# Dilated attention in a two-layer decoder trunk: near products wait for near values only, value loads and bias tables handled anew, products five steps behind their scores

## The chip, the cores and the metric

The kernel runs on the 8 NeuronCores of one Trainium2 chip. Each core computes one of the 8 batch elements alone; the cores share nothing but the memory's bandwidth. The metric is the device time in microseconds of the slowest core.

## The reference

```python
for layer in range(2):
    mod = silu(c) @ w_mod[layer] + b_mod[layer]            # shift, scale, gate for both sub-layers
    h = rms_norm(x) * (1 + scale_m) + shift_m              # (2048, 1024) per batch element
    q, k, v, rq, rk, rv, rg = split(h @ w_in[layer])       # 3 x 512, 2 x 256, 2 x 512 columns
    # group A: 8 heads x 64, QK-norm, causal, window of 128 steps in each of three dilations
    for window, dilation in ((128, 1), (512, 4), (2048, 16)):
        s = q.k / 8 + bias_table[t5_bucket(rel * dilation)]; p = exp(s)
    attn = (sum of p.v over the three) / (sum of p over the three)
    # group B: 4 heads of retention (rotary, decay, GroupNorm, swish gate)
    x = x + gate_m * (concat(attn, ret) @ w_out[layer])
    h = rms_norm(x) * (1 + scale_f) + shift_f
    f = swiglu(h) if layer == 0 else moe_top2_of_8(h)      # d_ff 2816, experts 3584
    x = x + gate_f * f
```

## The kernel before

The program is one static order of instructions. A helper class `K` records for each buffer who wrote and read it last; `op` and `dma` put the waits ahead of an instruction (`_deps`, `_wait`), and each engine and each issuing queue works strictly in program order. SyncE ("sp") issues the plain loads and stores, GpSimd ("pool") the loads that cast from f32 to bf16. A `dma` waits also for an earlier load into the same buffer. `P(name, ..., kb, n)` places a tile at a fixed address; a tile that lies over an older one waits for its users.

The work goes by in stages. (1) The modulation of layer 0: eight loads `wmi` of 1 MB, products on TensorE (lines 441 and 447), which give `nm.shift` and `nm.A`; `crep`, a cast of silu(c), is what these products stream against. `eb_table` makes exp of the bias for 3 dilations x 8 heads x 384 distances in `ebst`. (2) The first norm, 16 tiles of 128 tokens: `stats` (a square on ScalarE, two small operations of GpSimd), `apply` (two passes on VectorE), `turn` (eight transposes into one PSUM bank and a copy into `hT`). `HT[g]` is one buffer for four tiles of `hT`. (3) `eb_rows` writes the 24 rows of `ebst` to `ebscr` in memory and copies each 128 times into `ebrep`, so that a load with a row step of 383 elements turns a row into a 128 x 256 table `EB`. (4) `attention`: `vproj` computes the values of all 16 tiles (into `VV`, buffers `BVt`, with columns of ones beside them that give the denominators) and writes them to `vscr`; `load_v(c)` gathers from there, in five loads, the values of head pair c for dilations 4 and 16 (buffer `BVg[c % 2]`).

The heads run as four pairs c. A pair has two heads of 19 batches each: eight of near blocks (dilation 1) and eleven far ones, in the order three near, eleven far, five near. A step of the stream of 4 x 2 x 19 = 152 batches is `scores` (products of k and q, exp on ScalarE, times `EB` on VectorE into `pr`) of batch i and `pv` (products with the values) of batch i - LAG, with LAG = 3. Beside them run, by step, `proj` of the next pair's q and k (bank 6, with `sums` and `scale` one and two steps later), `load_c` (weights `wqk` and tables `EB` of the next pair), and `mod_step`, which works off the remaining modulation on VectorE from loads `wm` that SyncE issues. A product `pv` declares that it reads

```python
k.op("pe", mm, reads=[Bpr[y], BVg[z]] + BVt, writes=[PB[bank] for bank in ...])
```

Behind the attention come the retention with the output projection (`mixer`; `gated` needs powers from GpSimd), the dense FFN (`ffn_open` loads its first two groups of weights from within the retention's loop; `ffn` ends each half with down products, line 1184, and the next norm), layer 1 in the same way, and the experts (`moe`), which take the second half of the time.

## Time and profile before

| what | value |
|---|---|
| median of 3 runs (lowest, highest) | 3788.38 us (3781.92, 3816.22) |
| the profiled execution | 3776.37 us |
| its span, slowest core (3) | 3774.2 us |
| spans of cores 0 to 7 | 3764.1, 3758.8, 3751.3, 3774.2, 3703.3, 3734.5, 3677.8, 3682.0 us |
| mean granted TensorE clock, core 3 | 0.866 |
| TensorE busy | 2922.2 us, 77% |
| first product of the modulation | 37.12 us |
| last write of `A` | at 60.16 us, 0.69 us long |
| end of the values' projection, layer 0 | 154.6 us |
| first score product, layer 0 | 174.07 us |

A busy engine is not one that is used well: TensorE's clock has two levels, 2.4 and 1.2 GHz, and a granted clock of 0.50 over a stretch means that all of it ran at the lower one. A wait is shown with what ended it. Times are from the span's start on core 3.

### The profile page before, as it was taken

Reading aid. Unit: us, or ns where it says so; the run is one execution under the profiler, and the core shown is the slowest. Engines: PE = TensorE matmul, PEld = TensorE weight load, DVE = VectorE, ACT = ScalarE, POOL = GpSimd, SP = SyncE. Lnnn points to the kernel's source line nnn. Section 1 sums busy time; section 2 is a strip of 40 time slices with the busy share of each in tenths; the row PEclk is TensorE's granted clock in tenths of the full one; section 3 lists DMA queues with packets and bytes.
Section 4 is the critical chain, followed back from the end, with each engine's and each line's share of the span. In section 5 each row is a group of like instructions: output and inputs, shape, how many; then the busy total and the mean of one; then the engine's idle time right before and its main releaser. Section 6 shows DMA issues by size and latency. Waiting matters only on the chain.

```text
span 3774.2 us, 48947 instructions; the slowest of 8 cores (3677.8 to 3774.2 us)
## 1 busy us (share of the span) xinstructions
PE 2922.2 (77%) x16504; PEld 1479.3 (39%) x16513; DVE 1163.9 (31%) x1905; ACT 1072.5 (28%) x1949; POOL 510.6 (14%) x608
## 2 busy tenths in 40 slices
PE   3547798869999886798774588788856787688998
PEld 1212244434444432244332343346433543355464
DVE  2324465632321434444444111112111211112121
ACT  2324455521111143454442121213120211122120
POOL 2110001110100100000223112121211112020201
PEclk8767778989999987768886799899978999899999
DMA  6375331267432366311226886959496978979592
GB/s 189 62 165 132 108 105 57 90 143 114 105 74 45 96 153 138 85 38 56 75 70 116 155 122 101 173 83 169 80 165 94 169 101 133 134 117 156 79 137 35
DMA packets 310781, 417.18 MB, mean 111 GB/s; under 512 B 63740, under 2 KB 222996, under 8 KB 310449
## 3 DMA queue, kind: packets, MB, share of 16 engines
q0 software_dynamic: 215008, 254.14, 45.4%
q1 hardware_dynamic: 95442, 158.74, 13.5%
q8 instruction: 194, 3.18, 0.3%
q14 instruction: 137, 1.12, 0.1%
HBM read 576.69 MB, written 59.59 MB: 169 GB/s over the span
## 4 chain that ended last, share of the span: by engine, by line
PE 61%; DMA 17%; ACT 6%; issue 6%; DVE 5%; another core or an unknown queue 2%; POOL 1%; SPq 1%; DVEq 0%; ACTq 0%; POOLq 0%; PEldq 0%
PE ps L1510 16%; PE ps L1538 12%; PE ps L1153 8%; DMA t_w2m<-moe_w 4%; PE ps L1184 4%; DMA t_VV<-vscr 4%; PE ps L782 4%; PE ps L811 3%; PE ps L975 3%; PE ps L724 3%; PE ps L1071 3%; DMA t_ring<-moe_w 3%; DMA ebrep<-ebscr 3%; DVE t_gTm L1514 1%
## 5 line engine op out<-in xcount | busy, mean ns | idle before, releaser
L1510 PE MATMUL ps<-t_hgT,t_ring 128*128 128x0 bf16 (+1 forms) x5376 | 841.2, 317 | 212.6 <-DVE t_gTm L1514 107.7
L1510 PEld LDWEIGHTS ps<-t_hgT,t_ring 128*128 128x128 bf16 x5376 | 506.7, 100 | 547.7 <-issue 286.5
L1538 PE MATMUL ps<-t_w2m,t_gTm 128*128 128x512 bf16 x2016 | 448.7, 386 | 85.4 <-DMA t_w2m<-moe_w 85.0
L1514 DVE TENSOR_TENSOR t_gTm<-ps,t_sam 128x384 bf16<-128x384 f32 (+1 forms) x336 | 217.4, 647 | 834.5 <-ACT t_sam L1513 811.6
L1513 ACT ACTIVATE t_sam<-ps 128x384 bf16<-128x384 f32 (+1 forms) x336 | 186.6, 561 | 511.8 <-PE ps L1510 457.1
L1538 PEld LDWEIGHTS ps<-t_w2m,t_gTm 128*128 128x128 bf16 x2016 | 199.6, 99 | 331.9 <-issue 103.2
L1153 PE MATMUL ps<-hT,t_w 128*128 128x512 bf16 x1408 | 309.0, 383 | 1.3 <-ACT hT L539 1.3
L811 PE MATMUL ps<-t_pr,t_VV 128*128 128x32 bf16 (+2 forms) x1776 | 198.8, 270 | 102.1 <-DMA t_VV<-vscr 97.6
L1513 ACT ACT_TABLE_LOAD x56 | 71.8, 1283 | 723.8 <-PE ps L1510 717.3
L786 ACT ACTIVATE t_pr<-ps 128x512 bf16<-128x512 f32 (+1 forms) x304 | 177.2, 591 | 262.8 <-PE ps L782 243.3
L724 PE MATMUL ps<-hT,t_wqk 128*128 128x512 bf16 x512 | 163.3, 478 | 86.6 <-DMA t_wqk<-w_in 51.5
L794 DVE TENSOR_TENSOR t_pr<-t_pr,t_EB 128x512 bf16<-128x512 bf16 (+1 forms) x320 | 128.9, 405 | 304.8 <-ACT t_pr L786 258.7
L782 PE MATMUL ps<-t_qT,t_kT 64*128 64x256 bf16 (+1 forms) x768 | 204.1, 374 | 9.7 <-DVE t_kT L736 5.9
L975 PE MATMUL ps<-t_wr,hT 128*128 128x512 bf16 x768 | 190.6, 408 | 25.2 <-DVE t_m L985 19.4
L1153 PEld LDWEIGHTS ps<-hT,t_w 128*128 128x128 bf16 x1408 | 138.8, 99 | 170.9 <-issue 8.0
L811 PEld LDWEIGHTS ps<-t_pr,t_VV 128*128 128x128 bf16 x1776 | 119.0, 119 | 200.3 <-issue 190.4
L1543 DVE SCALAR_TENSOR_TENSOR t_ys<-ps,t_gts,s_gate 128x1024 f32<-128x1024 f32 x36 | 46.2, 1284 | 484.9 <-PE ps L1538 398.4
L1280 POOL DMA_DIRECT2D t_ring<-moe_w x98 | 86.9, 896 | 653.5 <-PE ps L1510 612.0
L1184 PE MATMUL ps<-t_w2s,t_gT 128*128 128x512 bf16 x704 | 155.6, 382 | 4.4 <-DVE t_gT L1157 4.4
L1157 DVE TENSOR_TENSOR t_gT<-ps,t_sa 128x512 bf16<-128x512 f32 x88 | 60.9, 692 | 253.2 <-ACT t_sa L1156 253.2
L1546 POOL DMA_INDIRECT out<-t_ys,t_idx x36 | 57.0, 1585 | 592.9 <-DVE t_ys L1543 489.3
L975 PEld LDWEIGHTS ps<-t_wr,hT 128*128 128x128 bf16 x768 | 77.7, 104 | 126.0 <-issue 53.6
(239 smaller groups left out, 2811.7 us busy)
## 6 DMA issues: line engine op xcount, KB each, us to landing
t_ring<-moe_w POOLq DMA_DIRECT2D x112, 1024.0 KB, 20.8
t_w2m<-moe_w POOLq DMA_DIRECT2D x56, 1024.0 KB, 28.1
t_wm<-w_mod SPq DMA_DIRECT2D x80, 512.0 KB, 3.9
t_w<-ffn_w POOLq DMA_DIRECT2D x20, 1024.0 KB, 9.1
t_wmi<-w_mod SPq DMA_DIRECT2D x8, 1024.0 KB, 16.4
t_n0x<-x SPq DMA_DIRECT2D x16, 512.0 KB, 6.1
t_wos<-w_out SPq DMA_DIRECT2D x16, 512.0 KB, 3.3
t_n1x<-x SPq DMA_DIRECT2D x16, 512.0 KB, 4.2
```

What stands on the lines that cost most here:

```text
L724: ins = e.matmul(ps[:, pb, :], lhsT=wqk[:, z, j, kc, :], rhs=hT[:, kc, tb * 512:(tb + 1) * 512], start=(kc == 0), stop=(kc == 7))
L782: ins = e.matmul(ps[:, sbk, o:o + w], lhsT=kT[rows, z, t0:t0 + 127 * d + 1:d], rhs=qT[rows, z, t0:t0 + (w - 1) * d + 1:d], start=True, sto ...
L786: k.op("act", lambda e: e.activation(out=pr[:, y, 0:W], in_=ps[:, sbk, 0:W], func=AF.Exp, scale=0.125), reads=[PB[sbk]], writes=[Bpr[y]])
L794: k.op("dve", lambda e: e.tensor_tensor(out=dst, in0=dst, in1=bcast_mid(tile_, n), op=ALU.mult), reads=[Bpr[y], BEB[z]], writes=[Bpr[y]])
L811: ins = e.matmul(ps[:, bank, c0:c0 + (w - 1) * d + 1:d], lhsT=VV[:, off + 64 * hh:off + 64 * hh + 128], rhs=pr[:, y, o:o + w], start=False ...
L975: ins = e.matmul(ps[:, bk, :], lhsT=hT[:, kc, t * 128:(t + 1) * 128], rhs=wr[:, kc, c0:c0 + 512], start=(kc == 0), stop=(kc == 7))
L1153: ins = e.matmul(ps[:, bk, :], lhsT=w13[:, z, w, kc, j * 128:(j + 1) * 128], rhs=hT[:, kc, tk:tk + 512], start=(kc == 0), stop=(kc == 7))
L1184: ins = e.matmul(ps[:, b0 + hf, :], lhsT=gT[:, fc, i * 128:(i + 1) * 128], rhs=w2s[:, fc, hf * 512:(hf + 1) * 512], start=(fc == 0), stop= ...
L1510: ins = e.matmul(o, lhsT=ring[:, s_, kc, j * 128:(j + 1) * 128], rhs=r, start=(kc == 0), stop=(kc == 7))
L1513: k.op("act", lambda e: e.activation(out=sa[z][:, 0:width], in_=ps[:, ba, 0:width], func=AF.Silu), reads=[PB[ba]], writes=[Bsa[z]], inc=inc)
L1514: k.op("dve", lambda e: e.tensor_tensor(out=gT[:, fc, c0:c0 + width], in0=ps[:, bb, 0:width], in1=sa[z][:, 0:width], op=ALU.mult), reads=[ ...
L1538: ins = e.matmul(ps[:, b0 + hf, :], lhsT=gT[:, fc, b * 128:(b + 1) * 128], rhs=w2s[:, fc, hf * 512:(hf + 1) * 512], start=(fc == 0), stop= ...
```

## The change

The diff is cut; left out are lines that only move with their function and the constant `anti`, a 128 x 128 identity with its rows in reverse order.

- `dma` gets `part=True`: the load doesn't wait for earlier loads into its own buffer. It is given to all but the first of: constants, gains, `wqk`, `Tt`, the gathers of `load_v`, the writes of `vscr`, `wr`, and the FFN's `w13`.
- The small loads of the start go behind the first `wmi` load, the other seven after them; the scaling of `gains` goes behind `crep`.
- `ebrep` and its 24 copies are gone. `load_c` loads 128 overlapping rows of 256 distances into `Tt`, and `flip` turns them over by a product with `anti` and copies the result into `EB` on ScalarE: three flips a pair, at steps 28, 31 and 34 of the pair before.
- `wv` is loaded ahead of the first norm, in layer 1 ahead of the last down products; `attention_open` (memsets, `load_c(0)`) runs from step 3 of the norm; `apply` lags `stats` by three steps, `turn` by four, and `vproj` by five, inside the norm's loop. In layer 1 eight `vproj` go beside the last two `turn`.
- A `pv` of near blocks waits for `BVt`, one of far blocks for `BVg[z]`. `load_v(c + 1)` is issued at the first `pv` of pair c, not at its first `scores`. LAG is 5, `pr` has 8 buffers in place of 4, and the projections stand 4 or 5 steps apart with `sums` and `scale` two and three steps later.

```diff
-    def dma(self, q, out, in_, reads=(), writes=(), issue=None):
+    def dma(self, q, out, in_, reads=(), writes=(), issue=None, part=False):
+
         E = self.E[q]
-        self._wait(E, self._deps(reads, writes))
         dst = writes[0]
+        deps = self._deps(reads, writes)
+        if part:
+            deps.pop("dma:" + dst.name, None)
+        self._wait(E, deps)
...
+    k.op("dve", lambda e: e.memset(tab[:], -30000.0), writes=[Btab_])
...
-    k.dma("pool", blk[:], cblk_d, writes=[B["constp"]])
+    k.dma("pool", blk[:], cblk_d, writes=[B["constp"]], part=True)
+    k.dma("pool", anti[:], dram["c_anti"], writes=[B["constp"]], part=True)
...
-    for h in range(8):
-        load_wmi(h)
-        if h == 0:
-            k.dma("sp", bmi[:], bmod_d[0:1, 0:2 * D], writes=[Bbmi])
+    load_wmi(0)
+    k.dma("sp", bmi[:], bmod_d[0:1, 0:2 * D], writes=[Bbmi])
     k.dma("sp", gains[:, 0:2], qg_d, writes=[B["gains"]])
-    k.dma("sp", gains[:, 2:4], kg_d, writes=[B["gains"]])
+    k.dma("sp", gains[:, 2:4], kg_d, writes=[B["gains"]], part=True)
     k.dma("sp", dec[:], cdec_d, writes=[B["oh"]])
-    k.dma("sp", gd[:], cgd_d, writes=[B["oh"]])
-    k.op("dve", lambda e: e.tensor_scalar(out=gains[:], in0=gains[:], scalar1=8.0, scalar2=None, op0=ALU.mult),
-         reads=[B["gains"]], writes=[B["gains"]])
-    k.op("dve", lambda e: e.memset(tab[:], -30000.0), writes=[Btab_])
+    k.dma("sp", gd[:], cgd_d, writes=[B["oh"]], part=True)
     k.dma("sp", tab[0:32, :], table_d, writes=[Btab_])
     k.dma("sp", oh[:], coh_d, writes=[Boh])
+    for h in range(1, 8):
+        load_wmi(h)
...
+    k.op("dve", lambda e: e.tensor_scalar(out=gains[:], in0=gains[:], scalar1=8.0, scalar2=None, op0=ALU.mult),
+         reads=[B["gains"]], writes=[B["gains"]])
...
-        for i_ in [8 * b_ + h for h in range(8) for b_ in range(3)]:
-            k.dma("sp", bass.AP(ebrep, i_ * 128 * 384, [[384, 128], [1, 384]]), bass.AP(ebscr, i_ * 384, [[0, 128], [1, 384]]),
-                  reads=[ebscr_buf], writes=[ebrep_buf])
...
-    eb_table()
-    nm.rest()
-    for i in range(NT + 2):
-        if i < NT:
-            nm.stats(i)
-        if 1 <= i <= NT:
-            nm.apply(i - 1)
-            if i - 1 + 8 < NT:
-                nm.load_x(i - 1 + 8)
-        if i >= 2:
-            nm.turn(i - 2, 6 + i % 2)
-    eb_rows()
...
-    def attention(l, mixT, BmixT, beside, load_wr):
...
+    vst = VV[:, 0:12288].rearrange("p (t n) -> p t n", t=16)
+    vpair = VV[:, 0:12288].rearrange("p (t c n) -> p t c n", t=16, c=4)
+    A = {}
...
+    def attention_weights(l):
+
+        wv, (Bwv,) = A["wv"] = P("wv", [128, 8, 512], BF16, 181)
+        k.dma("pool", wv[:], win_d[l, :, 1024:1536].rearrange("(c p) n -> p c n", p=128), writes=[Bwv])
+
+    def attention_open(l):
+
         retire(BVt + BVg)
-        wqk, Bwqk = P("wqk", [128, 2, 2, 8, 128], BF16, 112, n=2)
-        wv, (Bwv,) = P("wv", [128, 8, 512], BF16, 181)
-        EB, BEB = P("EB", [128, 2, 3, 2, 256], BF16, 120, n=2)
-        pr, Bpr = P("pr", [128, 4, 512], BF16, 189, n=4)
-        rsb, Brsb = zip(*(P("rsb%d" % q, [128, 512], F32, (132, 193)[q]) for q in range(2)))
-        Brsb = [b[0] for b in Brsb]
-        sqb, Bsqb = P("sqb", [128, 2, 512], BF16, 130, n=2)
-        rec, Brec = P("rec", [128, 2, 512], F32, 126, n=2)
-        vst = VV[:, 0:12288].rearrange("p (t n) -> p t n", t=16)
-        vpair = VV[:, 0:12288].rearrange("p (t c n) -> p t c n", t=16, c=4)
-
-        def vcols(t):
-
-            a = vpair[:, t]
-            d_ = [list(q) for q in a.ap]
-            return bass.AP(a.tensor, a.offset, [d_[0], d_[1], [128, 2], [1, 64]])
-        k.dma("pool", wv[:], win_d[l, :, 1024:1536].rearrange("(c p) n -> p c n", p=128), writes=[Bwv])
+        wv, (Bwv,) = A["wv"]
+        wqk, Bwqk = A["wqk"] = P("wqk", [128, 2, 2, 8, 128], BF16, 112, n=2)
+        Tt, (BTt,) = A["Tt"] = P("Tt", [128, 3, 512], BF16, 189)
+        A["v"] = 0
         for q in range(4):
...
         def load_c(c):
             z = c % 2
             for j in range(2):
-                k.dma("pool", wqk[:, z, j], win_d[l, :, j * 512 + c * 128:j * 512 + c * 128 + 128].rearrange("(c p) n -> p c n", p=128), writes=[Bwqk[z]])
-            for b in range(3):
-                for hh in range(2):
-                    i = b * 8 + c * 2 + hh
-                    k.dma("pool", EB[:, z, b, hh, :], bass.AP(ebrep, i * 128 * 384 + 127, [[383, 128], [1, 256]]), reads=[ebrep_buf], writes=[BEB[z]])
+                k.dma("pool", wqk[:, z, j], win_d[l, :, j * 512 + c * 128:j * 512 + c * 128 + 128].rearrange("(c p) n -> p c n", p=128), writes=[Bwqk[z]], part=j > 0)
+            for hh in range(2):
+                k.dma("pool", Tt[:, :, 256 * hh:256 * hh + 256], bass.AP(ebscr, (2 * c + hh) * 384, [[1, 128], [8 * 384, 3], [1, 256]]), reads=[ebscr_buf], writes=[BTt], part=hh > 0)
+        A["load_c"] = load_c
         load_c(0)
...
+        def vproj():
+            t = A["v"]
+            A["v"] += 1
             bk = 4 + t % 2
...
+                k.dma("sp", vscr[128 * t0:128 * (t0 + 4), :].rearrange("(t p) n -> p t n", p=128), vst[:, t0:t0 + 4, :], reads=[BVt[t // 4]], writes=[vscr_buf], part=t0 > 0)
...
+        A["vproj"] = vproj
+
+    eb_table()
+    nm.rest()
+    eb_rows()
+    attention_weights(0)
+    for i in range(NT + 5):
+        if i == 3:
+            attention_open(0)
+        if i < NT:
+            nm.stats(i)
+        if 3 <= i < NT + 3:
+            nm.apply(i - 3)
+            if i - 3 + 8 < NT:
+                nm.load_x(i - 3 + 8)
+        if 4 <= i < NT + 4:
+            nm.turn(i - 4, 6 + i % 2)
+        if i >= 5:
+            A["vproj"]()
+
+    def attention(l, mixT, BmixT, beside, load_wr):
+        qT, BqT = P("qT", [128, 2, S], BF16, 48, n=2)
+        kT, BkT = P("kT", [128, 2, S], BF16, 56, n=2)
+        vproj, load_c, flip_src = A["vproj"], A["load_c"], A["Tt"]
+        wqk, Bwqk = A["wqk"]
+        EB, BEB = P("EB", [128, 2, 3, 2, 256], BF16, 120, n=2)
+        rsb, Brsb = zip(*(P("rsb%d" % q, [128, 512], F32, (132, 193)[q]) for q in range(2)))
+        Brsb = [b[0] for b in Brsb]
+        sqb, Bsqb = P("sqb", [128, 2, 512], BF16, 130, n=2)
+        rec, Brec = P("rec", [128, 2, 512], F32, 126, n=2)
+        def flip(c, b, bank=None):
+
+            bank = next_bank() if bank is None else bank
+            k.op("pe", lambda e: e.matmul(ps[:, bank, :], lhsT=anti[:], rhs=flip_src[0][:, b], start=True, stop=True), reads=[B["constp"]] + flip_src[1], writes=[PB[bank]])
+            k.op("act", lambda e: e.copy(out=EB[:, c % 2, b].rearrange("p a n -> p (a n)"), in_=ps[:, bank, :]), reads=[PB[bank]], writes=[BEB[c % 2]])
+
...
+            for r in range(4):
+                k.dma("sp", d4[:, 4 * r:4 * r + 4, :], bass.AP(vscr.tensor, r * 768 + c * 192, [[3072, 128], [393216, 4], [1, 192]]), reads=[vscr_buf], writes=[BVg[z]], part=r > 0)
+            k.dma("sp", d16, bass.AP(vscr.tensor, c * 192, [[12288, 128], [768, 16], [1, 192]]), reads=[vscr_buf], writes=[BVg[z]], part=True)
...
         def scores(c, hh, bt, i):
-            z, sbk, y = c % 2, next_bank(), i % 4
+            z, sbk, y = c % 2, next_bank(), i % 8
...
-            k.op("pe", mm, reads=[Bpr[y], BVg[z]] + BVt, writes=[PB[bank] for bank in sorted(set(w_[1] for w_ in work))])
+            near = all(s_[0] == 0 for s_ in bt)
+            k.op("pe", mm, reads=[Bpr[y]] + (BVt if near else [BVg[z]]), writes=[PB[bank] for bank in sorted(set(w_[1] for w_ in work))])
...
-        for t in range(NT):
-            vproj(t)
+        while A["v"] < NT:
+            vproj()
         load_v(0)
+        pr, Bpr = P("pr", [128, 8, 512], BF16, 181, n=8)
...
-        LAG = 3
+        for b in range(3):
+            flip(0, b)
+        LAG = 5
         nb_ = len(bts)
         stream = [(c, hh, n) for c in range(4) for hh in range(2) for n in range(nb_)]
         work_beside = beside(mod_open(12 if l == 0 else 8), next_bank)
         due = {}
-        fill = []
+        fill = {}
         for i in range(len(stream) + LAG + 2):
             if i < len(stream):
                 c, hh, n = stream[i]
                 if hh == 0 and n == 0 and c + 1 < 4:
                     load_c(c + 1)
-                    load_v(c + 1)
-                    fill = [(c + 1, j, tb) for tb in range(4) for j in range(2)]
+                    for m, (tb, j) in enumerate((tb, j) for tb in range(4) for j in range(2)):
+                        fill[i + 1 + m * 9 // 2] = (c + 1, j, tb)
+                    for b in range(3):
+                        due.setdefault(i + 28 + 3 * b, []).append(lambda c=c, b=b: flip(c + 1, b))
                     if c == 1:
                         load_wr()
                 scores(c, hh, bts[n], i)
             for fn in due.pop(i, ()):
                 fn()
-            if fill and i % 4 == 1:
-                a_, b_ = proj(*fill.pop(0))
-                due.setdefault(i + 1, []).append(a_)
-                due.setdefault(i + 2, []).append(b_)
+            if i in fill:
+                a_, b_ = proj(*fill.pop(i))
+                due.setdefault(i + 2, []).append(a_)
+                due.setdefault(i + 3, []).append(b_)
             if 0 <= i - LAG < len(stream):
                 c, hh, n = stream[i - LAG]
+                if hh == 0 and n == 0 and c + 1 < 4:
+                    load_v(c + 1)
                 pv(c, hh, n, i - LAG)
...
         for w, src in ((0, w1_d), (1, w3_d)):
-            k.dma("pool", w13[:, z, w, :, 0:g * 128], src[:, c0 * 128:(c0 + g) * 128].rearrange("(c p) n -> p c n", p=128), writes=[Bw13[z]])
+            k.dma("pool", w13[:, z, w, :, 0:g * 128], src[:, c0 * 128:(c0 + g) * 128].rearrange("(c p) n -> p c n", p=128), writes=[Bw13[z]], part=w > 0)
...
+            if half == 1:
+                attention_weights(1)
...
+                if half == 1 and i == 8:
+                    attention_open(1)
                 if 2 <= i <= 9:
                     n2.turn(t - 2, i % 2)
+                if half == 1 and i in (8, 9):
+                    for _ in range(4):
+                        A["vproj"]()
...
```

## Rows read from the trace of the kernel before

**Rows 1.** The page, part 4: the chain that ended last, by engine.

```profile
PE 61%; DMA 17%; ACT 6%; issue 6%; DVE 5%; another core or an unknown queue 2%; POOL 1%; SPq 1%; DVEq 0%; ACTq 0%; POOLq 0%; PEldq 0%
```

**Rows 2.** Stages: window, us, busy per engine (instructions), clock, DMA, GB/s.

```profile
63.60:114.50 50.90, 16.14 (x128) 12.37 (x128) 40.55 (x33) 32.26 (x48) 35.12 (x34) 0.50 0.37 108
114.50:154.60 40.10, 29.80 (x129) 13.07 (x129) 7.58 (x10) 5.70 (x9) 0.88 (x1) 0.82 0.51 73
336.50:590.00 253.50, 210.92 (x1167) 90.93 (x1167) 140.51 (x267) 125.89 (x219) 7.34 (x12) 0.72 0.42 115
760.00:1303.00 543.00, 495.64 (x2389) 229.10 (x2387) 163.84 (x186) 100.92 (x173) 59.09 (x77) 0.95 0.47 96
1725.00:2040.00 315.00, 229.64 (x1385) 117.70 (x1386) 144.44 (x258) 149.13 (x348) 74.65 (x86) 0.84 0.23 73
```

**Rows 3.** TensorE's waits, 172 to 590 us: total, times, longest.

```profile
PE ps L724 <- DMA t_wqk<-w_in: 51.5, 1, 51.5
PE ps L811 <- DMA t_VV<-vscr: 47.8, 2, 24.1
PE ps L724 <- DVE t_qT L736: 14.0, 6, 5.3
```

**Rows 4.** SyncE's queue in order of time: start, us, what, count.

```profile
33.33 0.34 SPq L240 DMA_DIRECT2D s_gains<-k_gain  x1
...
91.73 100.73 SPq L240 DMA_DIRECT2D ebrep<-ebscr  x24
...
315.89 12.88 SPq L240 DMA_DIRECT2D t_VV<-vscr  x5
```

**Rows 5.** TensorE's timeline, where the second long stall ends.

```profile
336.51 0.58 PE L811 MATMUL ps<-t_pr,t_VV 128*128 128x256 bf16 x3 [23.68 <-DMA t_VV<-vscr]
```

**Rows 6.** Five microseconds of the start, columns as in rows 2.

```profile
25.00:30.00 5.00, 0.00 (x0) 0.00 (x0) 0.00 (x0) 0.00 (x0) 0.00 (x0) 1.00 1.04 321
```

**Rows 7.** TensorE's timeline: transposes and projections at either clock.

```profile
69.20 1.01 PE L536 MATMUL ps<-s_ident,t_n0hbf 128*128 128x128 bf16 x8 [6.29 <-DVE t_n0hbf L524]
...
158.29 1.89 PE L724 MATMUL ps<-hT,t_wqk 128*128 128x512 bf16 x8
...
262.28 3.57 PE L724 MATMUL ps<-hT,t_wqk 128*128 128x512 bf16 x8 [5.33 <-DVE t_qT L736]
...
1287.51 0.61 PE L536 MATMUL ps<-s_ident,t_n2hbf 128*128 128x128 bf16 x8
```

**Rows 8.** Groups by line, 60 to 175 us: busy, mean ns | idle.

```profile
L511 ACT ACTIVATE t_n0junk<-t_n0x 128x1024 bf16<-128x1024 f32 x16 | 16.9, 1058 | 0.2
L539 ACT COPY hT<-ps 128x1024 bf16<-128x1024 bf16 x16 | 16.2, 1012 | 18.6 <-PE ps L536 18.6
...
L699 ACT CAST t_VV<-ps 128x512 bf16<-128x512 f32 x8 | 4.7, 586 | 33.4 <-PE ps L694 33.4
...
L511 ACT ACTIVATION_READ_ACCUMULATOR t_n0junk<-t_n0x 128x1 f32 x16 | 3.1, 191 | 0.0
```

**Rows 9.** TensorE's waits, 1280 to 1400 us, then 1397 to 1725 us.

```profile
PE ps L536 <- DVE t_n2hbf L524: 8.2, 2, 5.1
...
PE ps L694 <- DMA t_wv<-w_in: 4.5, 1, 4.5
...
PE ps L811 <- DMA t_VV<-vscr: 49.8, 2, 27.3
PE ps L724 <- DVE t_qT L736: 10.5, 5, 4.6
```

**Rows 10.** GpSimd's timeline, then TensorE's waits, 740 to 1303 us.

```profile
770.38 1.89 POOL L240 DMA_DIRECT2D t_w<-ffn_w  x2 [8.21 <-DMA t_w<-ffn_w]
783.59 0.87 POOL L240 DMA_DIRECT2D t_w<-ffn_w  x1 [11.32 <-DMA t_w<-ffn_w]
...
PE ps L1039 <- DVE t_rett L1055: 19.1, 1, 19.1
```

**Rows 11.** A stretch of layer 0's last head pair, columns as in rows 2.

```profile
549.00:561.00 12.00, 12.00 (x47) 4.75 (x45) 10.69 (x22) 6.97 (x14) 0.00 (x0) 0.50 0.49 158
```

31 lines of the change are left out of this document (14 added, 17 removed).

## Prediction

> **What bounds the kernel now.** I first read the chain that ended last, by engine [rows 1]. TensorE carries 61% of it, DMA 17%: more than a sixth of the time is spent waiting for transfers, so the question is which of those waits the change touches. The table of stages [rows 2] shows where TensorE is not busy: the first norm (16.14 of 50.90 us busy), the values' projection behind it (29.80 of 40.10 us), the attention of layer 0. The list of waits [rows 3] names them: 51.5 us in one piece for the weights of the second head pair, 47.8 us in two pieces for the gathered values. The queue of SyncE [rows 4] shows why the first is so long: 24 copies into `ebrep`, one after another, 100.73 us in all; GpSimd's queue holds the tile loads out of `ebrep` ahead of the next `wqk`, so TensorE waits for weights that nobody has asked for yet. The second kind is seen at the step where it ends [rows 5]: the product that waited 23.68 us for values is a 256-column product of near blocks, the last batches of a head pair. It reads `BVt` only, and waits for `BVg` that `load_v(c + 1)` has just begun to refill. Layer 1 has the same kind of wait, 49.8 us in two pieces [rows 9].
>
> **The start.** Before, SyncE can issue the second gains load only at 33.33 us [rows 4], when the first has landed behind 8 MB of weights, and the cast `crep` waits behind the gains on VectorE, so the modulation begins at 37 us (table above) though the first weights are long there. After, the small loads come first and the products follow the weights as they land. `A` was ready at 60.16 + 0.69 = 60.85 us (table above). New: weights landed at about 31 us at the 321 GB/s of the saturated engines [rows 6]; `wv` (2.1 MB read) is now issued beside them, 2.1/0.321 = 6.5 us more; then the last block's products, two copies and the sum, 5 to 6 us (the four blocks took 60.85 - 37.12 = 23.7 us, 5.9 each). Estimate 43 us, gain 18 us, bounds 10 (products at half clock, x late) and 24 (`wv` hidden).
>
> **The norm loop with the values' projection inside.** Before, from `A` to the end of the projection is 154.6 - 60.85 = 93.8 us. After, projection t sits in the loop one step behind the transposes of t + 1. All four tiles of a group share one buffer `HT[t // 4]`, so projection t waits for the copy of t + 1 also, and the ScalarE copy of even tiles stands ahead of the next `stats`. Durations: transposes 0.61 us, eight products 1.89 us at the full clock (2.4 GHz), 3.57 us at half (1.2 GHz) [rows 7], its transposes 1.01 us; on ScalarE square 1.06 + 0.19, copy of `hT` 1.01, value copy 0.59 [rows 8]. With 0.1 us from engine to engine: an even tile costs copy 1.01 + projection 1.89 + value copy 0.59 + stats 1.25 + gaps = 5.06 us; an odd one inside its group projection + transposes + copy + gaps = 3.72; an odd one that ends a group 2.3. Four tiles: 5.06 + 3.72 + 5.06 + 2.3 = 16.1 us, 4.04 a tile; at half clock 6.73 + 5.8 + 6.73 + 3.65 = 22.9 us, 5.7 a tile. VectorE needs 40.55/16 = 2.5 us a tile [rows 2] and half a value copy, so it isn't the bound. TensorE would be busy 62% of the time at the full clock, 80% at half. The nearest row of this busy share is the retention stage of layer 1, 229.64 of 315 us at 0.84 [rows 2]; I take 4.6 us a tile. Ends: 10 us to the first copy (as before, `stats` 0 to 4 cover the lag of three, the memsets of VV fall before `apply`) + 16 x 4.6 + 2.6 = 86 us less some 4 as the first group starts full: 82. Gain 12 us; bounds +20 (full clock) and -6 (half).
>
> **The tables.** The 24 copies go. `eb_rows` keeps one small write, now ahead of the loop; four GpSimd issues (`wqk`, `Tt`) fall into the loop at step 3, about 3 us once, inside the three steps that `apply` now lags. `wqk` for pair 1 is issued right after the last `stats`, beside the first projections (8 x 1.89 us = 15 us), so the 51.5 us wait goes wholly: gain 51.5. In its place stand 24 flips in both layers: 24 products of 512 columns, 0.4 us each, and 24 ScalarE copies of 0.59 us, of which most fall beside products: cost 8 us (bounds 4 and 20: on ScalarE's 14 us all exposed and a few waits).
>
> **The values.** Near products wait for `BVt`, written long before. Far ones of pair c + 1 come 38 steps after `load_v(c + 1)`; `load_v(0)` has the eight first projections and eight steps (15 + 12 us) for its five parts, which took 12.88 us one after another [rows 4] and are now unordered. So both waits go whole: gain 47.8 and 49.8 us [rows 3, 9]. If the cover were gone, each pair would cost up to the 12.88 us.
>
> **Small waits.** The projections beside the stream wait for VectorE's scaling, 14.0 us in layer 0 [rows 3] and 10.5 in layer 1 [rows 9] on the side of q, and some 4 more each on that of k. Part of it (5.33 us once [rows 7]) is VectorE held by `mod_step` while SyncE works off the values' loads; that goes. Part is the bank 6 chain, and there the new spacing is no better (scaling one step later, projections 4 or 5 apart). I take half: 9 and 7 us; bounds 0 and all, 33. What distance five saves of the short waits for `pr` is in these 9. Five long stalls fewer also mean five fewer restarts at half clock, 3.57 instead of 1.89 us for a projection and the steps behind it: 2 us each, 10.
>
> **Layer 1's opening.** `wv` is loaded under the last down products, and eight projections go between the last transposes: the waits of 8.2 and 4.5 us [rows 9] could go. But the four memsets and the value copies stand behind the last norm on VectorE and hold banks 4 and 5; I take 5 us (0 to 10).
>
> **A wait outside attention.** In the retention of layer 0 `ffn_open` puts four loads into GpSimd's queue, and the second of each pair waited for the first to land: 8.21 and 11.32 us [rows 10]. Behind them stand the powers for `gated`, and TensorE stands 19.1 us for `t_rett` [rows 10]. With `part` there are four issues of 1 us in a row and no landing: gain 19.5 - 4 = 16 us (12 to 19). The weights land after 6 MB/0.3 = 20 us, before the first FFN product.
> The Trainium skill (DMA: Bandwidth & Descriptors, Anatomy of one DMA) gives such a load as 2.0 us and its bytes at 436 GB/s; for 1 and 2 MB that is 4.4 and 6.8 us, and by it the term would be an estimated 8 us and the sum 210. The rows' 8.21 and 11.32 differ from it, and they decide.
>
> **The sum.** 18 + 12 + 51.5 - 8 + 47.8 + 49.8 + 9 + 7 + 10 + 5 + 16 = 218 us. Against the profiled execution's 3776.4 us: 3558. The median shown is 12 us above that execution, so 3570 on that scale. All cores show the same waits within a few us, so the slowest stays slow; FFN and experts are untouched.
>
> **The rivals.**
> (1) The norm loop stays at half clock: 16 x 1.1 = 18 us less gain, 3588. For it: the whole norm ran at 0.50 [rows 2]; against: TensorE was busy 32% of it, and is to be busy 80%. 0.17.
> (2) The attention's stalls come back smaller, as waits for far values, for `wm` behind them on SyncE, or for bank 6 and flips: half of 97.6, the 16 of small waits and 10 more lost: 75 us, 3645. For it: VectorE hasn't much slack at the ends of pairs; against: all these transfers are issued a pair ahead. 0.13.
> (3) The denser stream gets more clock. The attention's stage from 336.5 us has a granted clock of 0.72 with 210.92 of 253.50 us busy [rows 2]; six pairs' streams 10 us shorter each: 3510. Against: the last stretch of layer 0 is busy 12.00 of 12.00 us at 0.50 [rows 11], without a stall to blame. 0.12.
> (4) The near batches weren't what waited (another order of semaphores), and 97.6 us stay: 3668. Against it [rows 5]. 0.05.
> (5) Slower than before: the stalls that go were the rest on which the clock lived. If the clock granted over the whole program falls, its 2302 us of TensorE on the chain (61% of 3774 [rows 1]) stretch by 0.866/c - 1; that eats the 218 us at c = 0.79, and below it the kernel is slower, 3800 at 0.785. For it: the half clock of that last stretch [rows 11]. Against: the FFN stage, dense for 543 us, holds 0.95 [rows 2]. 0.03.
>
> **From this to the numbers.** Forecast 0.50, and the rivals as given. Within the forecast the bounds of the terms add up to some 25 us either way. The range from 3505 to 3640 holds the forecast, (1), (3) and the better half of (2), 0.85 less the tails. One per cent is 38 us, about what a measurement of this kernel can tell from no change: only (5) is not faster by more, and part of it ends within; 0.96, 0.01, 0.03.
>
> **What would show it.** `A` ready near 43 us; the first score product near 145 us instead of 174; no wait of over 5 us for `t_VV` or `t_wqk`; loop steps of 4 to 5 us; TensorE's stream of layer 0 some 300 us long; in the retention before the FFN no 19 us wait for `t_rett`. The prediction is wrong if the loop takes 6 us a tile, if pairs' streams lengthen beyond 76 us, which is (253.5 - 24.1)/3 for the last three of layer 0 without the longest stall [rows 2, 3], or if the clock in FFN and experts falls.

## The result, and the profile after

The changed kernel is faster: 0.9579 times the kernel before, interval [0.9515, 0.9643]. Half of the cores ran at a lower clock in most executions of this measurement, so its plain median (3778.52 us, against 3802.30) says nothing of the change; the undisturbed executions took 3630.66 and 3621.22 us, and all times, comparisons and rows below leave disturbed executions and cores out. Two repetitions on other chips gave 0.96 [0.9495, 0.9706] and 0.9526 [0.949, 0.9562], with 3606 to 3621 us and 3599 to 3609 us. So the change gives 145 to 180 us where 218 were forecast. On the scale of the forecast (these ratios times 3788.38) the time is 3609 to 3637 us: at the upper end of the range from 3505 to 3640, and 39 to 67 us above the 3570.

Below are the stages, from the first product of one kind to the first of the next. "After" is the median of 8 cores of the first repetition; "core 3" is that core, in the profiled execution of before and in the first one of after. The forecast is the sum's terms, put where they act (of the 10 us of restarts, 6 in layer 0).

| stage, us | before, 8 cores | after, 8 cores | gain | before, core 3 | after, core 3 | gain | forecast |
|---|---|---|---|---|---|---|---|
| start to first score product | 174 | 145 | 29 | 174 | 145 | 29 | 30 |
| stream of layer 0 | 400 | 312 | 88 | 403 | 306 | 97 | 110 |
| retention and output | 233 | 219 | 14 | 237 | 220 | 17 | 16 |
| FFN | 481 | 482 | -1 | 483 | 482 | 1 | 0 |
| layer 1's opening | 65 | 57 | 8 | 65 | 57 | 8 | 5 |
| stream of layer 1 | 343 | 314 | 29 | 351 | 305 | 46 | 57 |
| retention of layer 1 | 415 | 417 | -2 | 417 | 416 | 1 | 0 |
| experts | 1623 | 1639 | -16 | 1644 | 1621 | 23 | 0 |

By the medians five stages came out as forecast within 3 us. Both streams fell short, 50 us together by the medians, 24 on core 3; and the experts' stage, which nothing in the change touches, became 16 us longer by the medians and 23 us shorter on core 3.

The chain that ended last, by engine, of the changed kernel on core 3 [rows 1]:

```profile
PE 69%; DMA 9%; ACT 7%; issue 6%; DVE 6%; POOL 1%; another core or an unknown queue 1%; SPq 1%; DVEq 0%; ACTq 0%; POOLq 0%; PEldq 0%
```

Of 17% of 3774 us on transfers 9% of 3551 are left: 642 us became 320. Next the stages that answer to rows 2, 9 and 11, core 3, the columns as there: start, loop with projections, first pair, stream of layer 0, retention, stream of layer 1.

```profile
10.00:50.50 40.50, 25.87 (x83) 5.46 (x84) 2.83 (x10) 3.52 (x6) 0.00 (x0) 1.00 1.01 275
50.50:125.30 74.80, 46.28 (x262) 22.43 (x261) 47.65 (x44) 39.87 (x60) 25.21 (x38) 0.82 0.60 136
125.30:145.20 19.90, 16.68 (x76) 7.16 (x75) 6.70 (x9) 15.10 (x27) 0.98 (x2) 0.99 0.64 150
145.20:451.00 305.80, 276.27 (x1553) 119.53 (x1553) 185.14 (x355) 166.22 (x294) 10.39 (x14) 0.75 0.55 135
451.00:671.00 220.00, 178.69 (x1176) 92.66 (x1177) 142.25 (x260) 120.34 (x323) 41.54 (x69) 0.94 0.37 102
1210.00:1515.00 305.00, 276.84 (x1546) 120.78 (x1545) 163.81 (x320) 167.26 (x295) 10.93 (x15) 0.74 0.45 103
```

TensorE is busy 276.27 of 305.80 us, in layer 1 276.84 of 305.00, so 29.5 and 28.2 us of waits are left in a stream. Before, the same streams on core 3 held 278.22 of 403.3 and 278.09 of 350.6 us. The busy time hardly moved; all of the gain is waits. Which waits are left, core 3, stream of layer 0 and then of layer 1 [rows 3, 9]:

```profile
PE ps L751 <- DVE t_qT L763: 19.6, 11, 3.5
PE ps L809 <- ACT t_pr L813: 4.0, 6, 1.0
PE ps L758 <- ACT t_sqb L754: 1.8, 2, 0.9
PE ps L618 <- DVE t_mev L607: 1.6, 1, 1.6
...
PE ps L751 <- DVE t_qT L763: 18.5, 10, 3.8
PE ps L809 <- ACT t_pr L813: 5.3, 7, 1.1
```

The waits for `t_wqk` and `t_VV` are gone from both streams. The projection's wait for VectorE's scaling (line 751 is 724 of before) did not halve: it rose from 14.0 to 19.6 us, and in layer 1 from the 10.5 of rows 9 (12.6 over the whole stream) to 18.5.

One of these waits differs from core to core. `t_mev` is what VectorE makes of the `wm` loads; no core waited for it in a stream of the kernel before, and in the repetition of the changed kernel the wait is 0 to 8.7 us in the stream of layer 0. Core 0 of that run, where VectorE itself waited 12.1 us for `t_wm`:

```profile
PE ps L618 <- DVE t_mev L607: 6.7, 1, 6.7
```

The start, TensorE's timeline of core 3, and below it the last write of `A` in VectorE's:

```profile
13.29 1.94 PE L446 MATMUL ps<-t_wmi,s_crep 128*32 128x512 f32 x8 [13.29 <-DVE s_gains L438]
23.00 1.94 PE L446 MATMUL ps<-t_wmi,s_crep 128*32 128x512 f32 x8 [7.78 <-DMA t_wmi<-w_mod]
29.87 3.64 PE L446 MATMUL ps<-t_wmi,s_crep 128*32 128x512 f32 x16
38.34 3.64 PE L446 MATMUL ps<-t_wmi,s_crep 128*32 128x512 f32 x16
44.91 1.92 PE L446 MATMUL ps<-t_wmi,s_crep 128*32 128x512 f32 x16
```

```profile
50.07 0.69 DVE L569 SCALAR_TENSOR_TENSOR t_n0A<-ps,t_n0normB 128x512 f32<-128x512 f32 x1 [2.22 <-PE ps L453]
```

The products begin at 13.29 us instead of 37.12, and `A` is ready at 50.76, not 43. From 23.00 us on nothing waits for a transfer; the blocks follow one another, and sixteen products take 3.64 us each time but the last, where they take 1.92.

### The profile page after: what moved, and what is told of

It reads as the page before. It is cut to its first block, busy times and chain, and to the rows that moved or that the text cites. A ratio compares the mean times of both kernels' runs of the same rounds, so it can differ in the third digit from the quotient of the medians.

```text
span 3751.6 us, 48806 instructions; the slowest of 8 cores (3551.2 to 3751.6 us)
## 1 busy us (share of the span) xinstructions
PE 3123.7 (83%) x16528; PEld 1508.3 (40%) x16537; DVE 1165.1 (31%) x1905; ACT 1084.2 (29%) x1973; POOL 485.4 (13%) x577
## 4 chain that ended last, share of the span: by engine, by line
PE 72%; DMA 7%; ACT 6%; issue 5%; DVE 5%; another core or an unknown queue 2%; POOL 1%; SPq 1%; ACTq 0%; DVEq 0%; POOLq 0%; PEldq 0%
PE ps L1552 17%; PE ps L1580 12%; PE ps L1188 10%; PE ps L1221 5%; PE ps L1010 5%; PE ps L751 4%; PE ps L838 4%; PE ps L809 4%; DMA t_w2m<-moe_w 3%; PE ps L1106 3%; PE ps L676 2%; DVE t_gTm L1556 2%; ACT t_sam L1555 2%; DMA t_ring<-moe_w 1%
## 5 line engine op out<-in xcount | busy, mean ns | idle before, releaser
L1552 PEld LDWEIGHTS ps<-t_hgT,t_ring 128*128 128x128 bf16 x5376 | 485.0, 100 | 584.4 <-issue 297.9
L1188 PE MATMUL ps<-hT,t_w 128*128 128x512 bf16 x1408 | 373.5, 439 | 1.3 <-ACT hT L544 1.3
L1188 PEld LDWEIGHTS ps<-hT,t_w 128*128 128x128 bf16 x1408 | 153.9, 109 | 220.1 <-issue 220.1
L1010 PE MATMUL ps<-t_wr,hT 128*128 128x512 bf16 x768 | 204.3, 431 | 25.3 <-DVE t_m L1020 23.8
L751 PE MATMUL ps<-hT,t_wqk 128*128 128x512 bf16 x512 | 189.9, 539 | 41.0 <-DVE t_qT L763 39.8
L838 PE MATMUL ps<-t_pr,t_VV 128*128 128x32 bf16 (+2 forms) x1776 | 216.4, 286 | 0.0
L1221 PE MATMUL ps<-t_w2s,t_gT 128*128 128x512 bf16 x704 | 188.2, 439 | 4.3 <-DVE t_gT L1192 4.3
L838 PEld LDWEIGHTS ps<-t_pr,t_VV 128*128 128x128 bf16 x1776 | 129.5, 123 | 103.7 <-issue 101.4
L1191 ACT ACTIVATE t_sa<-ps 128x512 bf16<-128x512 f32 x88 | 52.6, 597 | 321.4 <-PE ps L1188 321.4
## 6 DMA issues: line engine op xcount, KB each, us to landing
t_wmi<-w_mod SPq DMA_DIRECT2D x8, 1024.0 KB, 17.7
```

Source lines behind the costliest of these rows:

```text
L751: ins = e.matmul(ps[:, pb, :], lhsT=wqk[:, z, j, kc, :], rhs=hT[:, kc, tb * 512:(tb + 1) * 512], start=(kc == 0), stop=(kc == 7))
L838: ins = e.matmul(ps[:, bank, c0:c0 + (w - 1) * d + 1:d], lhsT=VV[:, off + 64 * hh:off + 64 * hh + 128], rhs=pr[:, y, o:o + w], start=False ...
L1010: ins = e.matmul(ps[:, bk, :], lhsT=hT[:, kc, t * 128:(t + 1) * 128], rhs=wr[:, kc, c0:c0 + 512], start=(kc == 0), stop=(kc == 7))
L1188: ins = e.matmul(ps[:, bk, :], lhsT=w13[:, z, w, kc, j * 128:(j + 1) * 128], rhs=hT[:, kc, tk:tk + 512], start=(kc == 0), stop=(kc == 7))
L1221: ins = e.matmul(ps[:, b0 + hf, :], lhsT=gT[:, fc, i * 128:(i + 1) * 128], rhs=w2s[:, fc, hf * 512:(hf + 1) * 512], start=(fc == 0), stop= ...
L1552: ins = e.matmul(o, lhsT=ring[:, s_, kc, j * 128:(j + 1) * 128], rhs=r, start=(kc == 0), stop=(kc == 7))
```

## The experiments

Each kernel is the changed one with an edit, unless it says "before with". "Streams" are the medians over 8 cores of the two streams, made as in the table. "Short waits" are the idle time of TensorE in a stream without its waits for transfers, again the median over 8 cores, for layer 0 and layer 1: 24 and 21 us in the kernel before, 33 and 33 in the changed one (first repetition).

**The changed kernel again.**

> The changed kernel itself, a second time, timed in rounds beside the kernel before. What is open: the sum forecast 218 us, the ratio of the first measurement is worth 160. On an undisturbed die the first profile shows the expert stage's first product 184 to 200 us earlier. Theory S (the streams were forecast too short, everything else holds): every core reaches its first expert product 180 to 200 us earlier and keeps that to the end, so the slowest core ends at 3776 - 190 = 3586 us. Rival X (the experts give part of it back): the first expert product comes 180 to 200 us earlier on all cores, but the expert stage is 20 to 60 us longer on the cores that were fastest before (4 to 7), and the slowest core ends near 3625.

0.96 [0.9495, 0.9706]; 3621, 3606, 3608 us beside 3741 to 3784 of the kernel before. Its stages are the table's. The medians of the stages ahead of the experts add up to 165 us. Core by core the first expert product came 138 to 181 us earlier, on all but one core less than either view expected (two of the cores took 20 us longer in the FFN than the others), and on cores 4 to 7 the experts' stage was 48 to 81 us longer than in the profile before. The end is close to what rival X said; whether that belongs to the kernel is asked again below.

**Before with the near products' wait alone.**

```diff
-            k.op("pe", mm, reads=[Bpr[y], BVg[z]] + BVt, writes=...)
+            near = all(s_[0] == 0 for s_ in bt)
+            k.op("pe", mm, reads=[Bpr[y]] + (BVt if near else [BVg[z]]), writes=...)
```

> The kernel before with one part alone: a product of near blocks waits for near values only; the gathered values are still loaded at the pair's first scores. The forecast's reason (the last near batches of a pair wait for the refill of the next) expects both long waits in each layer gone: 47.8 + 49.8 us of TensorE's waits for t_VV, streams of 355 and 302 us in place of 403 and 351 on core 3, the first expert product 95 us earlier. Rival (far batches were what waited, or the transfers come too late anyway): the waits move to a far product and no more than 30 us are gained.

0.9841 [0.9732, 0.995]; streams 364 and 306 instead of 400 and 343. The waits of the stream of layer 0, core 3:

```profile
PE ps L724 <- DMA t_wqk<-w_in: 52.1, 1, 52.1
PE ps L724 <- DVE t_qT L736: 17.7, 7, 7.4
PE ps L811 <- DVE t_pr L794: 5.2, 3, 3.3
PE ps L731 <- ACT t_sqb L727: 5.2, 5, 3.2
```

The 47.8 us for `t_VV` [rows 3] are gone, but only 36 us are gained (35 on core 3): `t_qT` went from 14.0 to 17.7, and `t_pr` and `t_sqb` (2.7 and 2.0 before) grew by 6 together. The short waits rose from 24 and 21 to 33 and 30 us. So the stall really was the near batches' wait. That VectorE and ScalarE had caught up with their work while TensorE stood, and no longer can, is my reading of the rows that grew.

**Before with the load's place alone.**

```diff
                     load_c(c + 1)
-                    load_v(c + 1)
...
                 c, hh, n = stream[i - LAG]
+                if hh == 0 and n == 0 and c + 1 < 4:
+                    load_v(c + 1)
                 pv(c, hh, n, i - LAG)
```

> The kernel before with another part alone: the gathered values of pair c + 1 are loaded at the first product of pair c with its values, behind all products of pair c - 1; every product still waits for near and gathered values. If the wait is only one of program order (the last near products stand behind a load that they don't need), moving the load cures it as well as splitting the wait: the same 95 us within 10 as with the split wait. If near products of pair c are held by something else in BVg, waits for t_VV of 10 us or more stay.

0.9794 [0.9693, 0.9894]; streams 364 and 304, no wait for `t_VV` over 1.2 us on any core; short waits 33 and 27. Each of the two edits alone takes the whole stall away: the last near batches of a pair then either don't ask for the gathers, or stand ahead of them in the order. Together they are not worth twice that. Both kernels keep the long `t_wqk` wait, 52.1 and 51.0 us on core 3; the changed kernel's stream of layer 0 is 312, so tables, flips, spacing and distance together are worth 52 us there, no more than that wait. In layer 1, which has no such wait, either edit alone gives a shorter stream (306 and 304 us) than the whole change (314): the rest of the change costs 8 to 10 us there. The forecast had nothing of this.

**The FFN's first weights in order again.**

```diff
-            k.dma("pool", w13[:, z, w, :, 0:g * 128], ..., writes=[Bw13[z]], part=w > 0)
+            k.dma("pool", w13[:, z, w, :, 0:g * 128], ..., writes=[Bw13[z]])
```

> The changed kernel with the FFN's w13 loads ordered again (the second of a pair waits for the first). The forecast's term of 16 us: TensorE waits some 19 us for t_rett again in the retention of layer 0, and that stage (first retention product to first FFN product) is 233 to 237 us in place of 218 to 220. Rival (the powers of GpSimd were held by something else): the stage stays within 4 us of the changed kernel's.

0.9649 [0.9542, 0.9755]; the retention takes 233 us again instead of 219, and every other stage is within 5 us of the changed kernel's. Core 3 of the changed kernel, GpSimd's queue, then three rows of this one and TensorE's wait in it [rows 10]:

```profile
634.08 3.62 POOL L244 DMA_DIRECT2D t_w<-ffn_w  x4
```

```profile
644.21 0.98 POOL L244 DMA_DIRECT2D t_w<-ffn_w  x1
653.70 1.76 POOL L244 DMA_DIRECT2D t_w<-ffn_w  x2 [8.50 <-DMA t_w<-ffn_w]
665.98 0.87 POOL L244 DMA_DIRECT2D t_w<-ffn_w  x1 [10.52 <-DMA t_w<-ffn_w]
```

```profile
PE ps L1074 <- DVE t_rett L1090: 21.0, 3, 18.4
```

Four issues in 3.62 us stand against four issues with 8.50 and 10.52 us of waiting for a landing between them. The term of 16 is 14 to 17 us.

**The kernel before again.**

> The kernel before a second time, with its trace. It settles rival X (the experts give part of the gain back on cores 4 to 7). In the first profile of before the experts took 1570 and 1576 us on cores 7 and 6, in the changed kernel's 1639 and 1657. If that difference belongs to the kernels, cores 6 and 7 are again under 1600 us here and the first expert product comes at 2100 to 2135 us. If the experts' time just varies by execution, cores 6 and 7 come out anywhere between 1570 and 1660, and the mean over the eight cores is 1620 to 1640 as in the changed kernel.

1.0027 [0.9981, 1.0072]. Its experts' stage was 1540 to 1648 us from core to core with the same instructions, 1601 on average; cores 6 and 7, with 1576 and 1570 us in the first profile, took 1617 and 1629 here. So a core's time in that stage changes from execution to execution by as much as rival X needed, and that stage sets how well a difference of 20 us can be seen at the end.

**The scaling of q and k one step earlier**, where it was before.

```diff
-                due.setdefault(i + 2, []).append(a_)
-                due.setdefault(i + 3, []).append(b_)
+                due.setdefault(i + 1, []).append(a_)
+                due.setdefault(i + 2, []).append(b_)
```

> The changed kernel with sums and scale of a projection one and two steps behind it, as before, in place of two and three; the spacing of 4 or 5 stays. Theory B (the small waits didn't shrink because bank 6 is given back a step later): the waits of the projection for t_qT fall from 18 to 19 us a stream to 12 or less, and each stream gets 5 to 10 us shorter. Rival V (they come from VectorE, which is behind by its modulation steps now that no stall lets it catch up): the waits stay within 3 us of 19, the streams within 4 us.

0.9482 [0.9443, 0.9521]; 3548 to 3557 us; streams 306 and 303 instead of 312 and 314. Core 3, stream of layer 0:

```profile
PE ps L751 <- DVE t_qT L763: 9.9, 6, 2.5
PE ps L758 <- ACT t_sqb L754: 5.4, 6, 1.8
```

The next projection waits in bank 6 for the scaling of the last one. Moved up a step it waits 9.9 instead of 19.6 us, and 3.6 of that come back as a wait for the squares. The short waits fall from 33 and 33 to 22 and 24 us. On core 3 the stream of layer 0 is no shorter for it, 306.1 for 306.2 us: 8.4 us less of waits met 8.3 us more of busy time, at a granted clock of 0.73 for 0.76. The gain is in the medians, where the busy time of layer 0 rose by 3 us and that of layer 1 fell by 2.

**Distance three instead of five.**

```diff
-        LAG = 5
+        LAG = 3
```

> The changed kernel with distance three in place of five, nothing else. The forecast gave the distance a share of 9 us in all. Theory D (distance hides the chain of scores, exp and tables): with three, the products wait for t_pr 4 to 7 us a stream, as in the kernel before with the split wait alone, and the streams are 5 to 10 us longer. Rival N (TensorE is busy 275 to 285 us of a stream at any distance, and what it doesn't wait for at one place it waits for at another): streams within 4 us.

0.9523 [0.9424, 0.9623]; 3550 to 3579 us; streams 314 and 311. Core 3:

```profile
PE ps L751 <- DVE t_qT L763: 24.9, 12, 9.3
PE ps L758 <- ACT t_sqb L754: 2.3, 3, 1.6
```

`t_qT` is 5 us longer here; of waits for `t_pr` only VectorE's is new, 1.9 us. Both views were half right. The short waits rose to 41 and 38 us, beside 32 and 32 of the next kernel on the same chip, whose streams have distance five; but TensorE's busy time fell to 272 and 273 us beside its 280 and 276, under what rival N allowed. So the distance does hide waits, some 6 to 9 us a stream, and the streams are as long as with five all the same. What made the products quicker is not shown; the granted clock is 0.75 to 0.78 here in the stream of layer 0 and 0.72 to 0.78 there.

**One buffer of `hT` for each tile**, for the values' projection in the norm's loop.

```diff
+    HTt = [k.buf("hTt%d" % t) for t in range(NT)]
...
-                 reads=[PB[bank]], writes=[HT[t // 4]])
+                 reads=[PB[bank]], writes=[HT[t // 4], HTt[t]])
...
-            k.op("pe", mm, reads=[Bwv, HT[t // 4]], writes=[PB[bk]])
+            k.op("pe", mm, reads=[Bwv, HTt[t]], writes=[PB[bk]])
```

> The changed kernel with one more buffer for each tile of hT: the values' projection of tile t waits for the copy of tile t alone, not for the last copy of its group of four. Forecast's model of the norm loop: the wait for the copy of t + 1 is 1.1 us and more on three tiles of four (19.5 us of TensorE's waits for hT in all), and without it a tile costs what ScalarE needs, 1.01 + 1.25 + 0.3 + gaps, or VectorE, 2.9 us. Then the loop takes 16 x 3.0 to 3.3 in place of 16 x 3.8, and the first score product comes at 132 to 137 us in place of 145. Rival (ScalarE's order sets the pace, hT's copy waits behind stats): 143 us or later.

The first score product comes at 125 us instead of 145, earlier than either view said. Its time at the end rests on one execution, 3570 us, and is left to the combination below. The loop on core 3, TensorE, the changed kernel and then this one:

```profile
86.76 3.52 PE L676 MATMUL ps<-t_wv,hT 128*128 128x512 bf16 x8 [2.33 <-ACT hT L544]
90.07 0.70 PE L541 MATMUL ps<-s_ident,t_n0hbf 128*128 128x128 bf16 x8
92.08 1.89 PE L676 MATMUL ps<-t_wv,hT 128*128 128x512 bf16 x8 [1.30 <-ACT hT L544]
93.81 0.61 PE L541 MATMUL ps<-s_ident,t_n0hbf 128*128 128x128 bf16 x8
94.25 1.89 PE L676 MATMUL ps<-t_wv,hT 128*128 128x512 bf16 x8
96.41 0.61 PE L541 MATMUL ps<-s_ident,t_n0hbf 128*128 128x128 bf16 x8 [0.26 <-DVE t_n0hbf L529]
98.75 1.89 PE L676 MATMUL ps<-t_wv,hT 128*128 128x512 bf16 x8 [1.74 <-ACT hT L544]
```

```profile
88.95 1.89 PE L677 MATMUL ps<-t_wv,hT 128*128 128x512 bf16 x8
91.11 0.61 PE L542 MATMUL ps<-s_ident,t_n0hbf 128*128 128x128 bf16 x8 [0.26 <-DVE t_n0hbf L530]
91.55 1.89 PE L677 MATMUL ps<-t_wv,hT 128*128 128x512 bf16 x8
94.38 0.61 PE L542 MATMUL ps<-s_ident,t_n0hbf 128*128 128x128 bf16 x8 [0.94 <-DVE t_n0hbf L530]
94.82 1.89 PE L677 MATMUL ps<-t_wv,hT 128*128 128x512 bf16 x8
96.97 0.61 PE L542 MATMUL ps<-s_ident,t_n0hbf 128*128 128x128 bf16 x8 [0.26 <-DVE t_n0hbf L530]
```

In the changed kernel a projection waits for the copy of the tile behind it; with the tile's own buffer the waits for `hT` are gone and VectorE's norm sets the pace: 91.11 to 96.97 us for two tiles, 2.9 each, where (125.3 - 59.1)/16 = 4.1 stood (59.12 us: the first transposes). Not all of the difference is waits. From the first transposes to the end of the projections the loop took 66.2 us and takes 48.4, and 5.2 of these 17.8 us are TensorE's own time, 39.62 us busy for 44.87: four projections of the changed kernel took 3.11 to 3.57 us, as the one at 86.76, and here only the first did (granted clock 0.93 for 0.84).

**Both of these edits.**

> The changed kernel with both edits that gained before: scaling of q and k one and two steps after its projection instead of two and three, and one hT buffer per tile for the values' projection. Theory A (they act in different stages, so they add): first score product at 125 us instead of 145, streams 304 and 302 us, retention and FFN as before the edits; together 20 + 17 = 37 us under the changed kernel, which is 3575 us, 0.95 or less of the kernel before. Rival T (only one of them counts at the end, since a denser start costs clock later): first score product at 125 but the stream of layer 0 back at 312 or more, together 17 to 20 us, 3592.

0.9415 [0.9367, 0.9463]; 3542 to 3583 us, 3567 on average beside 3605 of the changed kernel on the same chip. First score product at 127 us, streams 304 and 304: the two add, 38 us in all, and no clock is paid back for it. This is the best version found, some 215 us under the kernel before (3782 on average on that chip).

**Both parts about the values undone.**

```diff
-            k.op("pe", mm, reads=[Bpr[y]] + (BVt if near else [BVg[z]]), writes=...)
+            k.op("pe", mm, reads=[Bpr[y], BVg[z]] + BVt, writes=...)
...
                     load_c(c + 1)
+                    load_v(c + 1)
...
-                if hh == 0 and n == 0 and c + 1 < 4:
-                    load_v(c + 1)
                 pv(c, hh, n, i - LAG)
```

> The changed kernel with both parts about the values undone: every product with values waits for near and gathered values, and the gathers of the next pair are issued at its predecessor's first scores. The parts of a load stay unordered. Theory S (the stall is the whole gather and what the batches declared behind it wait for, as in the kernel before): two waits of 20 to 25 us for values in each layer, streams 348 and 350 instead of 312 and 313, 73 us in all. Rival O (each of the two waits was mostly the five gathers one behind the other; unordered they take a third): the two waits are there, but 8 to 12 us long, streams 325 to 330, 25 to 35 us in all; then the unordered gathers alone were worth more than half of this term.

0.9768 [0.972, 0.9815] beside 0.9526 of the changed kernel: 91 us. Streams 355 and 358 instead of 313 and 309 on the same chip. TensorE's timeline, then its waits, core 3, layer 0:

```profile
265.30 0.58 PE L838 MATMUL ps<-t_pr,t_VV 128*128 128x256 bf16 x3 [37.42 <-DMA t_VV<-vscr]
365.05 0.58 PE L838 MATMUL ps<-t_pr,t_VV 128*128 128x256 bf16 x3 [17.71 <-DMA t_VV<-vscr]
```

```profile
PE ps L838 <- DMA t_VV<-vscr: 55.1, 2, 37.4
PE ps L751 <- DVE t_qT L763: 20.5, 12, 3.5
```

The stall is back and longer than in rows 3, 55.1 for 47.8 us, so that the gathers no longer wait for one another did not shorten it. Their issues show a part of why: SyncE was busy 18.44 us with the five loads ahead of the longer wait,

```profile
230.04 18.44 SPq L244 DMA_DIRECT2D t_VV<-vscr  x5
```

against the 12.88 of the ordered ones in rows 4, and the product could start 16.8 us after the last of them was issued. Over the three sets of the stream it is a draw: 16.37, 18.44 and 9.24 us here, 18.94, 12.88 and 13.85 in the kernel before. `t_qT` stands at 20.5 us beside the stalls, so the late scaling costs this much with or without them. The wait for `t_mev` is gone on all eight cores. Distance three and the two single edits have next to none of it either, 0.3 us at most, so what brings it is open.

**Every flip done twice.**

```diff
-        def flip(c, b, bank=None):
+        def flip(c, b, bank=None, again=True):
...
+            if again:
+                flip(c, b, None, False)
```

> The changed kernel with every flip of a table done twice, product and ScalarE copy: 24 more products of 512 columns and 24 more copies of 0.59 us. Theory P (as predicted, 8 us for 24 flips, most of it beside other work): the streams lengthen by 3 to 4 us each and 1 us between projection and stream, 6 to 10 us in all. Rival F (the flips cost their full time on TensorE's bound stream and their copies delay exp): 7 to 10 us per layer, 14 to 20 in all. Rival Z (hidden): under 3 us.

0.9528 [0.9473, 0.9582]; 3602 to 3620 us, 3610 on average, 5 over the changed kernel. Streams 317 and 314 instead of 313 and 309, layer 1's opening 58 instead of 57; ScalarE has 20 table copies of 584 ns in the stream of layer 0 instead of 10 of 583. The 24 flips cost 5 to 10 us, though the stages' scatter of 3 us would also hide a cost of 3.

**The changed kernel a third time.**

> The changed kernel once more, beside the others of this call. Theory K (the experts' stage of 1641 us on average over the cores belonged to the chip of the first call): experts 1605 to 1620 on average, total 3575 to 3600. Rival M (it belongs to the kernel): 1635 to 1645 again while the kernel before shows 1600 to 1615, total 3605 to 3625.

0.9526 [0.949, 0.9562]; 3599 to 3609 us. The experts' stage of the first four cores was 1604 to 1647 us, 1622 on average. The total is between what the two views said, and the stage decides nothing: over all profiles here it is 1587 to 1642 us on average over the cores, 1616 and 1601 in the two of the kernel before, 1627, 1642 and 1622 in the three of the changed one (1627 and 1622 over four cores).

## Why the prediction was right or wrong

**The direction, and the mechanism of the long waits: right.** Neither the long `t_wqk` wait nor the `t_VV` waits are in the trace; rival 4 (other batches waited) is excluded by the near-wait and place experiments, rival 5 (a fall of the clock) by the mean granted clock, 0.893 on core 3 against 0.866. Rival 3 (a denser stream gets more clock and shortens the pairs) had the clock right, 0.75 for 0.69 in the stream of layer 0 on core 3, but the busy time fell by 2 us and not by 30.

**The size: short by 40 to 70 us, and most of it in one term, "Small waits".** This is the step that failed. I let them halve, 9 and 7 us of gain; they grew. They were 25.8 and 22.7 us on core 3 (the idle time of the two streams without the long waits) and became 29.5 and 28.2. Against the forecast of 16.8 and 15.7 that is 25.2 us, and the streams' shortfall on core 3 is 24. By the medians they were 24 and 21 us and became 33 and 33, 36 us over the forecast out of a shortfall of 50. I had written that the new spacing is no better and then taken half all the same. The scaling one step later is worse: put back, it took 19 us out of the short waits of both streams (medians) and shortened them by 7 and 11 us. The other cause is what the near-wait experiment showed: when a stall of TensorE goes, 9 us of short waits a stream appear beside it (35 us gained out of 47.8 on core 3). This is rival 2's mechanism at a third to a half of its size (25 or 36 of 75 us), and two of the places that it named are in the trace, bank 6 and `wm` (the wait for `t_mev`); the gathers are not.

**My own sign of being wrong came out.** I had named pairs beyond 76 us. The stream of layer 0 is 306/4 = 76.5 us a pair on core 3 and 312/4 = 78 by the medians. The 76 was even too generous: the window of rows 2 that I took it from runs to 590 us, and the stream ends at 577.4; to there the same sum gives 72.

**The values, 97.6 us.** Taken out of the kernel before alone, they gave 36 + 37 = 73; put back into the changed kernel, they cost 42 + 48 = 90, and 91 at the end. The term as a row was right and its share at the end depends on what else is late.

**Restarts, 10, and flips, -8.** The busy time of the two streams fell by 1.95 and 1.25 us on core 3, where these terms together say 2, but by the medians over the cores it rose by 1.7 and 1.3. The flips are about as dear as I said; no run shows the restarts.

**One core for all.** "All cores show the same waits within a few us" left out that core 3 had 403 and 351 us in its streams, against medians of 400 and 343: 11 us of forecast that the other cores could not give. After, core 3 was among the quickest, 306 and 305 against 312 and 314: 15 more. With the 24 of the small waits these are the 50 us by which the medians fall short. In the repetition some 7 of the 15 are again short waits, 29.5 and 29.1 us on core 3 against 33 and 33; why its products took less time too stays open.

**The start, 18: 10; the loop, 12: 19.** The two misses cancel, and 145 us as the place of the first score product was right for no good reason. I let the transfers set the end of the modulation; from 23.00 us on it was TensorE, 27 us for the blocks from there, with sixteen products in 3.64 us where 1.92 was possible; all four blocks had taken 23.7 before. That is the lower bound that I had named, 10 us. The loop's first transposes came 8.4 us behind `A` where I said 10, and from there a tile took 4.1 us, not 4.6: my own working had 4.04 for the full clock, and I had shaded it. Rival 1 (half clock in the loop) fell: 0.82 granted, and from 75 us on the projections took 1.89 us but for two of 3.52 and 3.11. What I named as the loop's limit, the shared buffer `HT[t // 4]`, is confirmed by the experiment that takes it away: 18 to 20 us, of which 5 are quicker products.

**`w13`, 16, and layer 1's opening, 5: 14 to 17, and 8.** Here the Trainium skill (DMA: Bandwidth & Descriptors, Anatomy of one DMA) had made the first term 8; ordered again, the loads waited 8.50 and 10.52 us, and the rows' price held.

**`wqk` and tables, 51.5.** The wait of 52.1 us is in the near-wait kernel and in no stream of the changed one, so the term is right as a row. No run has the tables alone. From 364 to 312 us between these two kernels is 52 us, but flips, spacing and distance are in it too, and together they gave nothing.

**What the end adds.** The sum of the stages ahead of the experts is 165 us by medians, against 218. The experts' stage gave -16 us (medians of one execution) and +23 us (core 3 of another) with the same kernel, and the same program spread over 100 us from core to core; since the slowest core is the metric, I take an error of some 15 us either way from there, and no experiment here says whether a part of it belongs to the change.

## What to carry to other kernels

A stall that goes gives back less than its row, as here 35 of 47.8 us, with 9 us of short waits in its place: list the short waits of the same stage and let them grow, not shrink, unless the change moves their own producer earlier. A load declared ahead of its buffer's last reader, or one buffer name for four tiles, shows in the waits as a transfer or a copy; for the load a finer name or a later place cured it, and one of them was enough; for the tiles a finer name did. Cost a chain of stages on the median core and on the slowest, and say which of them the number is for.
